# Two linked layers on one Trainium2 core: one of four weight sums per block-product group made in place by an adding transfer

## The chip, the core and the metric

The kernel runs on one core of a Trainium2 chip. Times are device microseconds (us) of one execution, without the host; lower is better. TensorE is called PE here, VectorE DVE, ScalarE ACT, GpSimd POOL and SyncE SP, as in the profile.

## The reference, cut to what matters

All of it is float32: 256 tokens of width 2048 go through a pooling mixer, a latent attention mixer, a hybrid mixer, a cross attention and a convolved feed-forward layer, one after the other, with norms and gates between. The change touches three of the many products with a weight matrix from memory:

```
out = (mixed * scale * silu(g)) @ pool_w_out        # 4096 x 2048, "pool_out"
out = (o * silu(g)) @ mla_w_out                     # 2048 x 2048, "mla_out"
out = (silu(conv(gate)) * val) @ w_down             # 5504 x 2048, "down"
```

## The kernel before, in words

**Products in three passes.** Each float32 weight tile is split into a high part (ACT copies it to float32r, w_hi) and a low part (DVE: raw - w_hi, w_lo). PE forms y_hi w_hi + y_hi w_lo + y_lo w_hi (function times, lines 961 to 965). A *unit* is a 512 KB tile of weights: two k tiles of 128 rows by 512 columns. SP loads units into the ring raw of 8 slots, each when the slot's last reader is done: it waits on w_lo for the product number that the table RELEASED gives (line 653). The rings w_hi and w_lo have 4 slots (RING), so ACT and DVE are at most four products ahead of PE.

**Groups of block products.** In the three products above a part of the inner dimension is done in groups: four units (B11, B12, B22, B21; two pairs of k tiles by two column chunks) meet a 2 x 2 block of the activations, and seven block products, each of half a plain unit's PE work, take the place of eight (Strassen's scheme in Winograd's form). That needs four sums of activations, made once, and four sums of weight tiles per group. In before, all four weight sums are DVE subtractions in place in raw (step_lo, lines 2465, 2467, 2469 and 2473), mixed with the seven low parts. ACT waits for each sum with w_sums (summed, line 1799). The block products go in the order B11, B22, T1, T3, B21, T2, T4 (function quad, line 1013; the names of the four sums are those of the change). Their results go into banks e1, e5, e6, e7 and the banks of the chunks; quads_mixed and quads_out add them up at the end of a pair of chunks.

There are 16 groups: 6 in pool_out (three per pair of chunks), 2 in mla_out and 8 in down (four per pair). The tables POOL_OUT, MLA_OUT and DOWN set the order: ten plain units stand before the first group of pool_out and of down, three before that of mla_out; between groups stand three plain units in pool_out, two in mla_out and four in down.

**POOL's queue.** layer_end(n) (line 3591) waits (n = 0: until PE has done eight products of pool_out; n = 1: attention heads done), loads post_gain (1024 KB), waits for it, and multiplies each chunk of the mixer's output by it when the chunk's squares are summed; for n = 1 it issues the loads of mem_features and mem_tokens (2048 KB each) at its first chunk. At the end of the kernel POOL waits for up, loads final_gain and multiplies the finished chunks. It is otherwise idle in these stages.

Of the kernel before, what the change touches and what calls it, by code (L numbers as in the profile page):

```python
# [71 lines left out]

POOL_QUADS = [20, 24, 28]
P0, P1, P2, P3 = ([("plain", c, (k, k + 1)) for k in range(0, 20, 2)] for c in range(NCH))
PQ = [[("quad", n, k)] for n, k in enumerate(POOL_QUADS)]
POOL_OUT = [P0[:9] + P1[:1] + PQ[0] + P1[1:4] + PQ[1] + P1[4:7] + PQ[2] + P1[7:] + P0[9:],
            P2[:4] + PQ[0] + P2[4:7] + PQ[1] + P2[7:9] + P3[:1] + PQ[2] + P2[9:] + P3[1:]]
# [3 lines left out]
D0, D1, D2, D3 = ([("plain", c, kts) for kts in DOWN_WHOLE] for c in range(NCH))  # L81
DOWN_ENDING = DOWN_WHOLE[-RING:]
DQ = [[("quad", n, k)] for n, k in enumerate(DOWN_QUADS)]
DOWN = [D0[:10] + DQ[0] + D1[:4] + DQ[1] + D1[4:8] + DQ[2] + D1[8:12] + DQ[3] + D1[12:] + D0[10:],
        D2[:4] + DQ[0] + D2[4:8] + DQ[1] + D2[8:12] + DQ[2] + D3[:4] + DQ[3] + D2[12:] + D3[4:]]
# [5 lines left out]
M2, M3 = ([("plain", c, (k, k + 1)) for k in range(0, 8, 2)] for c in (2, 3))  # L91
MQ = [[("quad", n, k)] for n, k in enumerate(MLA_OUT_QUADS)]
MLA_OUT = [[], M2[:3] + MQ[0] + M3[:2] + MQ[1] + M2[3:] + M3[2:]]


def quad_tables(first_unit, pairs, before):

    loads, released, quads_end, plain_end = [], [], [], {}
    last_quad = 0
    products = first_unit + before  # L100
    for p, steps in enumerate(pairs):
        for kind, c, kts in steps:
            if kind == "plain":
                loads.append((kts, c))
                released.append(products)
                products += 1
                plain_end[c] = products
            else:
                j1, j2 = (kts, kts + 1), (kts + 2, kts + 3)
                loads += [(j1, 2 * p), (j1, 2 * p + 1), (j2, 2 * p + 1), (j2, 2 * p)]  # L110
                released += [products + 3, products + 3, products + 5, products + 6]
                products += 7
                last_quad = products
        quads_end.append(last_quad)
    return loads, released, quads_end, plain_end
# [3 lines left out]
POOL_LOADS, POOL_RELEASED, POOL_QUADS_END, POOL_PLAIN_END = quad_tables(UNITS_END["pool"], POOL_OUT, 0)  # L119
SINCE_MLA_OUT = SINCE_POOL_OUT + 3 * len(MLA_OUT_QUADS)  # L120
MLA_OUT_PAIR = UNITS_END["heads"] + 16
MLA_OUT_LOADS, MLA_OUT_RELEASED, MLA_OUT_QUADS_END, MLA_OUT_PLAIN_END = quad_tables(MLA_OUT_PAIR, MLA_OUT, SINCE_POOL_OUT)
DOWN_LOADS, DOWN_RELEASED, DOWN_QUADS_END, DOWN_PLAIN_END = quad_tables(UNITS_END["up"], DOWN, SINCE_MLA_OUT)
# [8 lines left out]
assert POOL_RELEASED[-RAW:] == [UNITS_END["pool_out"] + SINCE_POOL_OUT - RAW + n for n in range(RAW)]  # L132
# [126 lines left out]
def build(nc, a, out):  # L259
# [191 lines left out]
    class Paired:  # L451

        def __init__(self, name, y, yh, yl, tiles, sums, sums_hi, sums_lo, quads, steps, loads, quads_end, plain_end, pairs_before):
# [3 lines left out]
            self.steps, self.loads, self.quads_end, self.plain_end, self.pairs_before = steps, loads, quads_end, plain_end, pairs_before  # L457
            self.both = len(steps[0]) > 0
# [13 lines left out]
        def blocks(self, j, tt):  # L472
# [10 lines left out]
    pool_out = Paired("pool_out", y32, yh, yl, POOL_Y, psums, psums_hi, psums_lo, POOL_QUADS, POOL_OUT, POOL_LOADS,  # L483
                      POOL_QUADS_END, POOL_PLAIN_END, 0)
    down = Paired("down", fy, fyh, fyl, DOWN_Y, fsums, fsums_hi, fsums_lo, DOWN_QUADS, DOWN, DOWN_LOADS,
                  DOWN_QUADS_END, DOWN_PLAIN_END, 3)
    msums, msums_lo, msums_hi = (arena(f"mla_y_sums{n}", off, [128, 4, len(MLA_OUT_QUADS), 2, 128], dt)
                                 for n, off, dt in (("", 81920, F32), ("_lo", 81920, F32R), ("_hi", 90112, F32R)))
    mla_out = Paired("mla_out", None, xh, xl, [], msums, [msums_hi[:, m] for m in range(4)], msums_lo, MLA_OUT_QUADS, MLA_OUT,
                     MLA_OUT_LOADS, MLA_OUT_QUADS_END, MLA_OUT_PLAIN_END, 1)  # L490
# [228 lines left out]
    def _(pe):  # L719
# [238 lines left out]
        pe.wait_ge(S("ident_in"), 16)  # L958
# [8 lines left out]
        def paired(x, split, ending=()):  # L967

            def pair(p):
# [21 lines left out]
                def plain(c, kts):  # L991
# [3 lines left out]
                    for n, k in enumerate(kts):  # L995
                        cols = slice(n * 512, n * 512 + 512)
                        for tt in range(2):
                            tok = slice(tt * 128, tt * 128 + 128)
                            last = times(x.bank(c, tt), x.yh[:, k, tok], x.yl[:, k, tok], wh[:, cols], wl[:, cols],
                                         begins((c, tt)), (c, kts) == final[c] and n == len(kts) - 1)  # L1000
# [3 lines left out]
                def block(dst, name, yh_, yl_, final=False):  # L1004

                    wh, wl = weight_slot()
                    for n in range(2):
                        cols = slice(n * 512, n * 512 + 512)
                        last = times(dst, yh_[:, n], yl_[:, n], wh[:, cols], wl[:, cols], n == 0 and begins(name), final and n == 1)
# [3 lines left out]
                def quad(q, k):  # L1013

                    e1, e5, e6, e7 = x.quad_banks(p)
                    c, last = 2 * p, q == len(x.quads) - 1
                    y_ready(k)
                    y1, y2 = slice(k, k + 2), slice(k + 2, k + 4)
                    t0, t1 = slice(0, 128), slice(128, 256)
                    block(e1, "e1", x.yh[:, y1, t0], x.yl[:, y1, t0], last)  # L1020
                    block(x.bank(c + 1, 0), (c + 1, 0), x.sums_hi[2][:, q], x.sums_lo[:, 2, q])
                    if x.both:
                        block(e5, "e5", x.yh[:, y1, t1], x.yl[:, y1, t1], last)
                    else:
                        block(e5, "e5", x.sums_hi[3][:, q], x.sums_lo[:, 3, q], last)
                    block(e7, "e7", x.sums_hi[0][:, q], x.sums_lo[:, 0, q], last)
                    block(x.bank(c, 0), (c, 0), x.yh[:, y2, t0], x.yl[:, y2, t0])
                    block(e6, "e6", x.sums_hi[1][:, q], x.sums_lo[:, 1, q], last)
                    block(x.bank(c, 1), (c, 1), x.yh[:, y2, t1], x.yl[:, y2, t1])
                    t.add("unit", 4)  # L1030
                    t.add("more", -4)
# [31 lines left out]
                final = {c: (c, kts) for kind, c, kts in x.steps[p] if kind == "plain"}  # L1063
# [8 lines left out]
                steps = x.steps[p][:-len(ending)] if p == 1 and ending else x.steps[p]  # L1072
                for kind, c, kts in steps:
                    if (kind == "quad" or c == 2 * p + 1) and begins("all sets"):
                        for s in range(2):
                            pe.wait_ge(S(f"mm_free{s}"), t.at(f"set{s}", 1))
                    if kind == "plain":
                        plain(c, kts)
                    else:
                        if c == 0 and not x.both:  # L1080
                            pe.wait_ge(S(split), len(POOL_Y) + 1)
                        elif c == 0 and p == 0:
                            pe.wait_ge(S(split), x.tiles.index("sums") + 1)
                        quad(c, kts)
# [516 lines left out]
    def _(act):  # L1601
# [191 lines left out]
        def loaded(n, cols=1024):  # L1793

            u = t.n["unit"] + n
# [3 lines left out]
        def summed(n, k):  # L1799

            act.wait_ge(S("w_sums"), t.n.get("w_sums", 0) + k)
            return raw[:, (t.n["unit"] + n) % RAW, :]

        def step_hi(kind, kts):

            if kind == "plain":
                product_hi(loaded(0, 512 * len(kts)))
                t.add("unit")
                t.add("more", -1)
            else:  # L1810
                product_hi(loaded(0))
                product_hi(loaded(2))
                product_hi(summed(0, 1))
                product_hi(summed(1, 2))
                product_hi(loaded(3))
                product_hi(summed(2, 3))
                product_hi(summed(3, 4))
                t.add("unit", 4)
                t.add("more", -4)
                t.add("w_sums", 4)  # L1820
# [86 lines left out]
        for n, (kind, _, kts) in enumerate(POOL_OUT[0]):  # L1907
            if n >= 6:
                step_hi(kind, kts)
# [10 lines left out]
        for n, (kind, _, kts) in enumerate(POOL_OUT[1]):  # L1920
            step_hi(kind, kts)
# [175 lines left out]
        for n, (kind, _, kts) in enumerate(MLA_OUT[1]):  # L2097
            if n >= LEAD:
                step_hi(kind, kts)
# [288 lines left out]
        for n, (kind, _, kts) in enumerate(DOWN[0]):  # L2388
            if n >= 6:
                step_hi(kind, kts)  # L2390
            if n in DOWN_Y_STEPS:
                y_hi(DOWN_Y_STEPS[n])
        for n, (kind, _, kts) in enumerate(DOWN[1]):
            step_hi(kind, kts)
# [26 lines left out]
    def _(dve):  # L2421
# [32 lines left out]
        def step_lo(kind, kts):  # L2454

            u = t.n["unit"]
            if kind == "plain":
                product_lo(raw[:, u % RAW, 0:512 * len(kts)])
                t.add("unit")
                t.add("more", -1)  # L2460
                return
            b11, b12, b22, b21 = (raw[:, (u + n) % RAW, :] for n in range(4))
# [1235 lines left out]
```

## Time and profile before

| | |
|---|---|
| median of 3 runs | 2436.18 us (2436.09 to 2437.14) |
| profiled execution, first to last instruction (span) | 2434.2 us |
| its own time outside the span | not listed apart; the median lies 2.0 us above the span |
| PE / DVE / ACT / POOL busy | 100% / 71% / 56% / 3% of the span |
| HBM traffic over the span | 185 GB/s |
| granted PE clock | 0.999 |

A row of the profile's groups reads: line, engine, operation, output <- inputs, shapes, count | busy us, mean ns of one | idle time of the engine before them and what ended it. A time in a timeline counts from the start of the span, and a DMA's time to landing from its issue. PE's matmuls overlap in the pipeline, so the mean of one is longer than the distance between two. PEld is the weight load, which overlaps PE.

### The profile page before, as it was taken

The numbers are of one execution on the slowest core, as the hardware profiler recorded it, in microseconds if no ns is written. First come the engines' busy times: TensorE is split into PE (matmuls) and PEld (weight loads), VectorE is DVE, ScalarE is ACT, GpSimd is POOL, SyncE is SP. The second block draws the span as 40 slices with busy tenths as digits, with TensorE's granted clock in tenths as the row PEclk, the third lists the DMA queues.
The fourth block names the chain that finished last, engine by engine and source line by source line (L and its number), as shares of the span: only waits on it lengthen the run. The fifth ranks groups of instructions, "written<-read, shape, count | busy, mean of one in ns | idle before, by whom it ended". The sixth has DMA issues, their size and how long they took to land.

```text
span 2434.2 us, 33996 instructions
## 1 busy us (share of the span) xinstructions
PE 2423.9 (100%) x12679; PEld 2084.6 (86%) x12679; DVE 1720.3 (71%) x2083; ACT 1373.7 (56%) x1823; POOL 64.7 (3%) x79
## 2 busy tenths in 40 slices
PE   9999999999999999999999999999999999999998
PEld 8888888888889999888888888888988888888887
DVE  7675757899765656796756667665767657679887
ACT  6444444556656666565755556565644545455555
POOL 0000000001100000010000000000000000000001
PEclk9999999999999999999999999999999999999999
DMA  8666666565555554565585554454565565656654
GB/s 314 199 189 185 188 189 183 188 218 199 180 175 181 179 158 147 211 212 189 165 235 163 161 171 151 164 178 154 172 191 180 189 190 180 191 169 205 220 184 145
DMA packets 234595, 453.03 MB, mean 186 GB/s; under 512 B 14929, under 2 KB 60417, under 8 KB 233324
## 3 DMA queue, kind: packets, MB, share of 16 engines
q1 hardware_dynamic: 230960, 435.94, 55.9%
q0 software_dynamic: 3120, 14.90, 1.7%
q10 hardware_dynamic: 396, 0.59, 0.2%
q8 instruction: 75, 1.23, 0.2%
q14 instruction: 44, 0.36, 0.0%
HBM read 448.68 MB, written 2.69 MB: 185 GB/s over the span
## 4 chain that ended last, share of the span: by engine, by line
PE 99%; DVE 1%; ACT 0%; issue 0%; ACTq 0%; DVEq 0%
PE ps L813 25%; PE ps L815 13%; PE ps L779 12%; PE ps L781 12%; PE ps L780 12%; PE ps L963 6%; PE ps L964 6%; PE ps L965 6%; PE ps L737 1%; PE ps L844 1%; PE ps L846 1%; PE ps L845 1%; PE ps L1443 1%; PE ps L1214 0%; PE ps L1202 0%; PE ps L1401 0%
## 5 line engine op out<-in xcount | busy, mean ns | idle before, releaser
L2443 DVE TENSOR_TENSOR w_lo<-raw,w_hi 128x1024 fp32r<-128x1024 f32 x689 | 842.1, 1228 | 466.7 <-ACT w_hi L1613 446.8
L1613 ACT ACTIVATE w_hi<-raw 128x1024 fp32r<-128x1024 f32 x689 | 726.8, 1060 | 650.9 <-PE ps L815 357.7
L813 PE MATMUL ps<-x_hi_lo,w_hi 128*128 128x512 f32 x2336 | 821.0, 394 | 0.0
L815 PE MATMUL ps<-x_hi_lo,w_lo 128*128 128x256 f32 x2336 | 660.7, 283 | 0.0
L813 PEld LDWEIGHTS ps<-x_hi_lo,w_hi 128*128 128x128 f32 x2336 | 438.8, 188 | 101.2
L779 PE MATMUL ps<-w_hi,x_hi_lo 128*128 128x512 f32 (+3 forms) x1184 | 461.9, 390 | 0.0
L781 PE MATMUL ps<-w_hi,x_hi_lo 128*128 128x512 f32 (+3 forms) x1184 | 453.7, 383 | 0.0
L780 PE MATMUL ps<-w_lo,x_hi_lo 128*128 128x512 f32 (+3 forms) x1184 | 452.7, 382 | 0.0
L815 PEld LDWEIGHTS ps<-x_hi_lo,w_lo 128*128 128x128 f32 x2336 | 439.3, 188 | 0.0
L1790 ACT ACTIVATE w_hi<-raw 128x1024 fp32r<-128x1024 f32 (+1 forms) x201 | 209.4, 1051 | 169.8 <-PE ps L965 152.2
L2451 DVE TENSOR_TENSOR w_lo<-raw,w_hi 128x1024 fp32r<-128x1024 f32 (+1 forms) x201 | 243.2, 1228 | 35.4 <-ACT w_hi L1790 35.1
L781 PEld LDWEIGHTS ps<-w_hi,x_hi_lo 128*128 128x128 f32 x1184 | 222.5, 188 | 39.1
L779 PEld LDWEIGHTS ps<-w_hi,x_hi_lo 128*128 128x128 f32 x1184 | 222.8, 188 | 36.5 <-issue 1.2
L780 PEld LDWEIGHTS ps<-w_lo,x_hi_lo 128*128 128x128 f32 x1184 | 222.9, 188 | 35.9
L964 PE MATMUL ps<-w_lo,ffn_y_hi 128*128 128x512 f32 (+1 forms) x283 | 111.0, 392 | 0.0
L965 PE MATMUL ps<-w_hi,ffn_y_lo 128*128 128x512 f32 (+1 forms) x283 | 111.0, 392 | 0.0
L963 PE MATMUL ps<-w_hi,ffn_y_hi 128*128 128x512 f32 (+1 forms) x283 | 111.0, 392 | 0.0
L813 PE MATMUL ps<-pooled_hi_lo,w_hi 128*128 128x512 f32 x256 | 90.0, 393 | 0.0
L963 PE MATMUL ps<-w_hi,pool_y_hi 128*128 128x512 f32 x208 | 82.3, 396 | 0.0
L964 PE MATMUL ps<-w_lo,pool_y_hi 128*128 128x512 f32 x208 | 82.1, 395 | 0.0
L965 PE MATMUL ps<-w_hi,pool_y_lo 128*128 128x512 f32 x208 | 82.1, 395 | 0.0
L815 PE MATMUL ps<-pooled_hi_lo,w_lo 128*128 128x256 f32 x256 | 72.4, 283 | 0.0
(469 smaller groups left out, 2711.9 us busy)
## 6 DMA issues: line engine op xcount, KB each, us to landing
raw<-in_w_up SPq DMA_DIRECT2D x160, 512.0 KB, 3.9
raw<-in_pool_w_in SPq DMA_DIRECT2D x126, 512.0 KB, 3.8
raw<-in_w_in SPq DMA_DIRECT2D x96, 480.0 KB, 3.8
raw<-in_w_down SPq DMA_DIRECT2D x84, 512.0 KB, 5.1
raw<-in_pool_w_out SPq DMA_DIRECT2D x64, 512.0 KB, 4.8
raw<-in_ple_w_gate SPq DMA_DIRECT2D x64, 512.0 KB, 4.3
raw<-in_mla_w_in SPq DMA_DIRECT2D x56, 448.0 KB, 3.5
raw<-in_pool_w_group SPq DMA_DIRECT2D x32, 512.0 KB, 4.1
```

The costliest lines, as they stand in the source:

```text
L779: pe.matmul(dst, xhi[:, k, tok], wh, start=k == units[0][0], stop=False)
L780: pe.matmul(dst, xhi[:, k, tok], wl, start=False, stop=False)
L781: last = pe.matmul(dst, xlo[:, k, tok], wh, start=False, stop=k == units[-1][-1])
L813: pe.matmul(bank, w_hi[:, slot, cols], xs[:, k].rearrange("p s n -> p (s n)"), start=k == 0, stop=False, skip_group_check=True)
L815: last = pe.matmul(bank[:, 0:T], w_lo[:, slot, cols], xs[:, k, 0, :], start=False, stop=k == nkt - 1, skip_group_check=True)
L963: pe.matmul(dst, yh_, wh, start=first, stop=False)
L964: pe.matmul(dst, yh_, wl, start=False, stop=False)
L965: return pe.matmul(dst, yl_, wh, start=False, stop=final)
L1613: act.activation(w_hi[:, t.slot(), :], raw[:, slot, :], ACT.Copy).then_inc(S("w_hi"), 1)
L1790: act.activation(w_hi[:, t.slot(), 0:cols], src, ACT.Copy).then_inc(S("w_hi"), 1)
L2443: dve.tensor_tensor(w_lo[:, t.slot(), :], raw[:, u % RAW, :], w_hi[:, t.slot(), :].bitcast(F32), ALU.subtract)\
L2451: dve.tensor_tensor(w_lo[:, t.slot(), 0:cols], src, w_hi[:, t.slot(), 0:cols].bitcast(F32), ALU.subtract).then_inc(S("w_lo"), 1)
```

## The change

Per group, the sum of the first row's two tiles, B12 + B11, is made by a DMA on POOL's queue that adds tile B11 into tile B12 (weight_sums; issued when both tiles have landed and the adding transfer before has too; its landing counts w_added). DVE makes the other three sums; it waits for w_added after the low part of B22, and ACT waits for it before T1's high part. SP loads B12 ahead of B11. The block products go B11, B22, T1, B21, T3, T2, T4. Signs of activation sums and of the final additions are turned to fit. The causal mask's load shares a semaphore with the identity's, so PE and DVE wait for both. The lists of steps are flattened to one entry per block product. weight_sums stands behind the load of post_gain in layer_end (for pool_out and for mla_out) and behind the load of final_gain (for down). The diff, cut:

```diff
+PARTS = ("B11", "B22", "T1", "B21", "T3", "T2", "T4")
+SLOT_OF = {"B12": 0, "T1": 0, "B11": 1, "T3": 1, "B22": 2, "T2": 2, "B21": 3, "T4": 3}
+LAST_USE = ("T1", "T3", "T2", "T4")
...
+def quads_at(first_tiles):
+
+    return [[(part, n, k) for part in PARTS] for n, k in enumerate(first_tiles)]
...
-                loads += [(j1, 2 * p), (j1, 2 * p + 1), (j2, 2 * p + 1), (j2, 2 * p)]
-                released += [products + 3, products + 3, products + 5, products + 6]
...
+                loads += [(j1, 2 * p + 1), (j1, 2 * p), (j2, 2 * p + 1), (j2, 2 * p)]
+                released += [at[part] for part in LAST_USE]
...
-        pe.wait_ge(S("ident_in"), 16)
+        pe.wait_ge(S("ident_in"), 32)
...
+                    if name == "B11":
+                        y_ready(k)
+                        t.add("unit", 4)
+                        t.add("more", -4)
+                        block(i, e1, "e1", x.yh[:, y1, t0], x.yl[:, y1, t0])
+                    elif name == "B22":
+                        block(i, x.bank(c + 1, 0), (c + 1, 0), x.sums_hi[2][:, q], x.sums_lo[:, 2, q])
+                    elif name == "B21":
+                        block(i, x.bank(c, 0), (c, 0), x.yh[:, y2, t0], x.yl[:, y2, t0])
+                    elif name == "T1" and x.both:
+                        block(i, e5, "e5", x.yh[:, y1, t1], x.yl[:, y1, t1])
+                    elif name == "T1":
+                        block(i, e5, "e5", x.sums_hi[3][:, q], x.sums_lo[:, 3, q])
+                    elif name == "T3":
+                        block(i, e7, "e7", x.sums_hi[0][:, q], x.sums_lo[:, 0, q])
+                    elif name == "T2":
+                        block(i, e6, "e6", x.sums_hi[1][:, q], x.sums_lo[:, 1, q])
...
+        def step_hi(entry):
+
+            for kind, _, kts, u in entry:
+                if kind == "plain":
+                    product_hi(loaded(u, 512 * len(kts)))
+                elif kind in ("B11", "B22", "B21"):
+                    product_hi(loaded(u + SLOT_OF[kind]))
+                else:
+                    if kind == "T1":
+                        act.wait_ge(S("w_added"), 16 * (t.n.get("quad", 0) + 1))
+                    else:
+                        act.wait_ge(S("w_sums"), 3 * t.n.get("quad", 0) + {"T2": 1, "T3": 2, "T4": 3}[kind])
+                    product_hi(raw[:, (u + SLOT_OF[kind]) % RAW, :])
...
-            product_lo(b11)
-            dve.wait_ge(S(f"raw_full{(u + 1) % RAW}"), 16 * ((u + 1) // RAW + 1))
-            dve.tensor_tensor(b11, b12, b11, ALU.subtract).then_inc(S("w_sums"), 1)
-            product_lo(b22)
-            dve.tensor_tensor(b12, b22, b12, ALU.subtract).then_inc(S("w_sums"), 1)
-            product_lo(b11)
-            dve.tensor_tensor(b22, b22, b11, ALU.subtract).then_inc(S("w_sums"), 1)
-            product_lo(b12)
-            product_lo(b21)
-            dve.wait_ge(S("w_sums"), t.n.get("w_sums", 0) + 3)
-            dve.tensor_tensor(b21, b21, b22, ALU.subtract).then_inc(S("w_sums"), 1)
-            product_lo(b22)
...
+                b12, b11, b22, b21 = (raw[:, (u + n) % RAW, :] for n in range(4))
+                product_lo(raw[:, (u + SLOT_OF[kind]) % RAW, :])
+                if kind == "B22":
+                    dve.wait_ge(S("w_added"), 16 * (t.n.get("quad", 0) + 1))
+                    dve.tensor_tensor(b22, b22, b12, ALU.add).then_inc(S("w_sums"), 1)
+                elif kind == "T1":
+                    dve.wait_ge(S("w_sums"), 3 * t.n.get("quad", 0) + 1)
+                    dve.tensor_tensor(b11, b22, b11, ALU.subtract).then_inc(S("w_sums"), 1)
+                elif kind == "T3":
+                    dve.tensor_tensor(b21, b21, b22, ALU.add).then_inc(S("w_sums"), 1)
...
+        def weight_sums(x):
+
+            for u in x.weight_sums:
+                b12, b11 = (raw[:, (u + n) % RAW, :] for n in range(2))
+                for v in (u, u + 1):
+                    pool.wait_ge(S(f"raw_full{v % RAW}"), 16 * (v // RAW + 1))
+                if t.n["quad"]:
+                    pool.wait_ge(S("w_added"), 16 * t.n["quad"])
+                pool.dma_start(b12, b11, accum_op=ALU.add).then_inc(S("w_added"), 16)
+                t.add("quad")
...
             load(pgain, a["post_norm"][n:n + 1, :].broadcast_to([128, D]), "post_gain_in")
+            weight_sums(mla_out if n else pool_out)
             pool.wait_ge(S("post_gain_in"), 16 * (n + 1))
...
         products(pool, "up")
         load(fgain, a["norm_final_2"].unsqueeze(0).broadcast_to([128, D]), "final_gain_in")
+        weight_sums(down)
         pool.wait_ge(S("final_gain_in"), 16)
...
-                step(dve.tensor_tensor(o1[1], o1[0], e6, ALU.add))
+                step(dve.tensor_tensor(o1[1], e6, o1[0], ALU.subtract))
```

## Rows read from the trace of the kernel before

**Rows 1.** The page: span, busy time and share by engine.
```profile
span 2434.2 us, 33996 instructions
...
PE 2423.9 (100%) x12679; PEld 2084.6 (86%) x12679; DVE 1720.3 (71%) x2083; ACT 1373.7 (56%) x1823; POOL 64.7 (3%) x79
```

**Rows 2.** Paired stages in windows: us, busy by engine, clock, DMA share, GB/s.
```profile
457.00:632.00 175.00, 175.00 (x754) 141.41 (x753) 156.78 (x158) 100.39 (x110) 12.71 (x8) 1.00 0.61 206
...
2197.00:2427.00 230.00, 229.80 (x1000) 186.57 (x998) 201.22 (x190) 129.00 (x140) 9.77 (x7) 1.00 0.56 187
```

**Rows 3.** Line L963 by source: what its engine sat idle for.
```profile
its engine sat idle before it (us, times) until:
  DVE w_lo L2451: 0.4, 1
  DVE w_lo L2443: 0.3, 1
```

**Rows 4.** DVE groups by shape: line, op, count, busy us, mean ns, idle.
```profile
L2465 DVE TENSOR_TENSOR raw<-raw 128x1024 f32<-128x1024 f32 x16 | 19.5, 1218 | 0.0
```

**Rows 5.** DVE's timeline over the first group: start us, us, line, count.
```profile
479.61 2.35 DVE L2451 TENSOR_TENSOR w_lo<-raw,w_hi 128x1024 fp32r<-128x1024 f32 x2
...
483.01 1.22 DVE L2451 TENSOR_TENSOR w_lo<-raw,w_hi 128x1024 fp32r<-128x1024 f32 x1
484.15 1.22 DVE L2467 TENSOR_TENSOR raw<-raw 128x1024 f32<-128x1024 f32 x1
...
494.45 1.22 DVE L2451 TENSOR_TENSOR w_lo<-raw,w_hi 128x1024 fp32r<-128x1024 f32 x1
```

**Rows 6.** PE's weight loads there: first for T1, first after the group.
```profile
488.40 0.19 PEld L963 LDWEIGHTS ps<-w_hi,pool_y_hi 128*128 128x128 f32 x1
...
495.73 0.19 PEld L963 LDWEIGHTS ps<-w_hi,pool_y_hi 128*128 128x128 f32 x1 [0.37 <-DVE w_lo L2451]
```

**Rows 7.** POOL's timeline: start us, us, line, and idle before.
```profile
480.69 0.53 POOL L3589 DMA_DIRECT2D post_gain<-in_post_norm  x1 [450.10 <-PE ps L965]
...
1009.02 0.54 POOL L3589 DMA_DIRECT2D post_gain<-in_post_norm  x1
1019.49 0.53 POOL L3589 DMA_DIRECT2D mem_features<-in_mem_features  x1 [9.94 <-ACT mixer_out L1710]
```

**Rows 8.** DMA issues, to landing (us): at 480.6, 1009 and 1024; all.
```profile
post_gain<-in_post_norm POOLq DMA_DIRECT2D x1, 1024.0 KB, 7.0
...
post_gain<-in_post_norm POOLq DMA_DIRECT2D x1, 1024.0 KB, 4.9
...
raw<-in_mla_w_out SPq DMA_DIRECT2D x5, 512.0 KB, 10.3
...
raw<-in_w_down SPq DMA_DIRECT2D x84, 512.0 KB, 5.1
raw<-in_pool_w_out SPq DMA_DIRECT2D x64, 512.0 KB, 4.8
...
mem_features<-in_mem_features POOLq DMA_DIRECT2D x1, 2048.0 KB, 8.3
...
final_gain<-in_norm_final POOLq DMA_DIRECT2D x1, 1024.0 KB, 8.3
...
hybrid_qk_T<-junk POOLq DMA_DIRECT2D x16, 1.0 KB, 1.5
```

**Rows 9.** Two groups later in down: DVE timeline, then a PE weight load.
```profile
2347.05 1.23 DVE L2451 TENSOR_TENSOR w_lo<-raw,w_hi 128x1024 fp32r<-128x1024 f32 x1 [0.17 <-ACT w_hi L1790]
...
2362.14 1.22 DVE L2467 TENSOR_TENSOR raw<-raw 128x1024 f32<-128x1024 f32 x1
...
2367.78 0.19 PEld L963 LDWEIGHTS ps<-w_hi,ffn_y_hi 128*128 128x128 f32 x1
```

**Rows 10.** DVE's timeline in mla_out's pair.
```profile
1045.59 1.22 DVE L2451 TENSOR_TENSOR w_lo<-raw,w_hi 128x1024 fp32r<-128x1024 f32 x1
...
1059.03 1.22 DVE L2451 TENSOR_TENSOR w_lo<-raw,w_hi 128x1024 fp32r<-128x1024 f32 x1
```

More of the change, by code:

```diff
@@ L90 @@
 MLA_OUT_QUADS = [8, 12]
[L91 to L98, printed above, removed]
+M2, M3 = ([plain(c, (k, k + 1)) for k in range(0, 8, 2)] for c in (2, 3))
+MQ = quads_at(MLA_OUT_QUADS)
+MLA_OUT = [[], M2[:3] + MQ[:1] + M3[:2] + MQ[1:] + M2[3:] + M3[2:]]
@@ L99, in quad_tables, with paired_tables @@
+def paired_tables(first_unit, pairs, before):
+    loads, released, quads_end, plain_end, steps, units = [], [], [], {}, [], []
     last_quad = 0
     products = first_unit + before
-    for p, steps in enumerate(pairs):
-        for kind, c, kts in steps:
+    for p, pair in enumerate(pairs):
+        steps.append([])
+        for entry in pair:
+            unit = first_unit + len(loads)
+            steps[-1].append([(kind, c, kts, unit) for kind, c, kts in entry])
+            at = {kind: products + n for n, (kind, _, _) in enumerate(entry)}
+            products += len(entry)
+            kind, c, kts = entry[0]
@@ L131 @@
 assert all(r <= UNITS_END["mla_out"] + SINCE_MLA_OUT - RAW + n for n, r in enumerate(MLA_OUT_RELEASED[-RAW:]))
-assert POOL_RELEASED[-RAW:] == [UNITS_END["pool_out"] + SINCE_POOL_OUT - RAW + n for n in range(RAW)]
+assert all(r <= UNITS_END["pool_out"] + SINCE_POOL_OUT - RAW + n for n, r in enumerate(POOL_RELEASED[-RAW:]))
 HEAD_CHUNKS = [("gate", 3), ("k", 0), ("v", 0), ("k", 1), ("gate", 4), ("v", 1), ("k", 2), ("gate", 5), ("v", 2),
@@ L1061, in turned_ending @@
                     t.add("unit", len(ending))
-                final = {c: (c, kts) for kind, c, kts in x.steps[p] if kind == "plain"}
+                banks = {"B11": ["e1"], "T1": ["e5"], "T2": ["e6"], "T3": ["e7"], "B22": [(2 * p + 1, 0)], "B21": [(2 * p, 0)], "T4": [(2 * p, 1)]}
+                parts = [at for entry in x.steps[p] for at in entry]
+                closing = {bank: i for i, (kind, c, _, _) in enumerate(parts) for bank in banks.get(kind, [(c, 0), (c, 1)])}
                 if p == 0:
@@ L1071, in pair @@
                     pe.wait_ge(S(f"mm_free{s}"), t.at(f"set{s}", 1))
-                steps = x.steps[p][:-len(ending)] if p == 1 and ending else x.steps[p]
-                for kind, c, kts in steps:
-                    if (kind == "quad" or c == 2 * p + 1) and begins("all sets"):
+                steps = parts[:-len(ending)] if p == 1 and ending else parts
+                for i, (kind, c, kts, _) in enumerate(steps):
+                    if (kind != "plain" or c == 2 * p + 1) and begins("all sets"):
                         for s in range(2):
@@ L1077, in pair @@
                     if kind == "plain":
-                        plain(c, kts)
+                        plain(i, c, kts)
                     else:
-                        if c == 0 and not x.both:
+                        if kind == "B11" and c == 0 and not x.both:
                             pe.wait_ge(S(split), len(POOL_Y) + 1)
-                        elif c == 0 and p == 0:
+                        elif kind == "B11" and c == 0 and p == 0:
                             pe.wait_ge(S(split), x.tiles.index("sums") + 1)
-                        quad(c, kts)
+                        part(i, kind, c, kts)
                 if p == 1 and ending:
@@ L1919, in _ @@
                 y_hi(n - 4)
-        for n, (kind, _, kts) in enumerate(POOL_OUT[1]):
-            step_hi(kind, kts)
+        for n, entry in enumerate(pool_out.steps[1]):
+            step_hi(entry)
             if n == 15:
@@ L2925, in _ @@
             quads_mixed(0, n)
-        for n, (kind, _, kts) in enumerate(POOL_OUT[1]):
-            step_lo(kind, kts)
+        for n, entry in enumerate(pool_out.steps[1]):
+            step_lo(entry)
             if n == 1:
@@ L3536, in _ @@
                 quads_out(0, n - 28)
-        for n, (kind, _, kts) in enumerate(DOWN[1]):
-            step_lo(kind, kts)
+        for n, entry in enumerate(down.steps[1]):
+            step_lo(entry)
             if n == 0:
```

175 lines of the change are left out of this document (75 added, 100 removed).

## The prediction

> **What bounds the kernel now.** I read the page first: TensorE (PE) is busy for 2423.9 of the 2434.2 us span [rows 1]. A share of 100% alone does not prove a bound, since matmuls are pipelined, so I looked next at the stages that the change touches. In the windows of pool_out and down, PE is busy all the time at a granted clock of 1.00, VectorE (DVE) 157 of 175 us and 201 of 230 us, the DMA engines 0.61 and 0.56 [rows 2]. Then I asked what the product line L963 waited for: 0.7 us in the whole kernel, both waits for w_lo from DVE [rows 3]. So PE sets the end, and the work that the change takes from DVE lies beside PE. The most that it can give back is the 0.7 us of waits. Everything that makes a product's weights late, on the other hand, is paid in full, because PE never catches up.
>
> **The change, part by part.** *Removed:* one of the four DVE sums in each of the 16 groups, 16 x 1.218 = 19.5 us of DVE [rows 4]. All of it lies under PE's matmuls. Worth on the path: the 0.37 us stall before the first unit behind group 1 [rows 6], perhaps; its cover is PE's own work. The swapped signs of the sums and the wait on the identity's semaphore are the same operations: nothing.
>
> *Order.* B21 now comes before T3 on PE, ACT and DVE, seven products as before. On SP the slots come free after products 2, 4, 5 and 6 instead of 3, 3, 5 and 6. The slot of T1 is free a product earlier, the next one a product later. The second slot is where the next group's second tile goes in down, so this sits inside the window reckoned below; otherwise I put it at zero.
>
> *Added:* 16 transfers on POOL's DMA queue, each adding one 512 KB tile into another, and three kinds of waits: POOL for both tiles (and the transfer before), ACT and DVE for the landing. Behind DVE's wait stands all that PE needs: the T2 sum, then the low parts of T1, B21, T3 and so on. The question for each group is whether the transfer lands in time.
>
> *Group 1 of pool_out* is the special one. POOL reaches its first transfer only when eight products of pool_out are done, and behind the load of post_gain, which is issued at 480.69 and takes 0.53 us to issue [rows 7]. Both tiles have then long landed. This post_gain is 1024 KB and lands 7.0 us after its issue [rows 8], at 487.7. The adding transfer is issued at about 481.2 on the same queue, and I take it to move after post_gain. When is it needed? DVE has done B11 and B22 low by 483.1 (in before, B22's began at 483.01 behind one sum that now is gone [rows 5]). From the landing X DVE then has, before the first whole unit behind the group, ten operations: sum, T1, sum, B21, T3, sum, T2, T4, a y part, the unit. They follow each other at 484.15 - 483.01 = 1.14 us [rows 5]. With 0.2 us for the semaphore, the last end and PE, that unit starts at X + 11.6. In before it started at 495.73 [rows 6]. So the loss is X - 484.1. (The nearer product T1, first weights at 488.40 [rows 6], needs only X + 2.5, so the end of the group decides.)
>
> *X.* No accumulating transfer is in the trace. mem_features (2048 KB) landed in 8.3 us and the second post_gain (1024 KB) in 4.9 [rows 8]: one more MB costs 3.4 us. An adding transfer reads two tiles and writes one. Counted as half a MB it costs 1.7 us behind post_gain, as 1.5 MB 5.1 us. I take 2.5 us, between 1.7 and the 3.4 of one MB, because SP's queue runs dry while DVE waits (DVE frees the slots). X = 490.2, loss 6.1 us. Ends: 489.4 gives 5.3 and 492.8 gives 8.7.
>
> Behind that rests the order on the queue. The Trainium skill (DMA: Bandwidth & Descriptors, "Two DMAs through the same engine are not ordered") says that inside one queue of one engine descriptors start in order, though completion isn't guaranteed in order. By that rule the transfer can't begin before post_gain's pieces; here no row shows two such transfers well enough to prove it. The same page ("Anatomy of one DMA") fits 2.0 us + bytes/436 GB/s, an estimate of 3.2 us for 512 KB. By that alone X would be 484.4 and the loss 0.3 us; but its 4.4 us for 1 MB is below both post_gain rows, 7.0 and 4.9.
>
> *The other 15 groups.* In down, a group's second tile can be asked for when T3's low part of the group before is done, 2347.05 + 1.23 = 2348.3 [rows 9], and lands 5.1 us later, at 2353.4. T1's first weights are loaded at 2367.78 [rows 9], so X may be 2365.3. The unit behind the group starts five products later; those take 495.73 - 0.37 - 488.40 = 6.96 us [rows 6], so at 2374.7. It wants nine DVE operations (no y part), 10.5 us, so X may be 2364.2: a window of 10.8 us. DVE itself would wait from 2362.1 on without harm. POOL-queue transfers took 1.5 us (1 KB) to 8.3 us (1 MB, final_gain; or 2 MB) [rows 8], an adding one estimated at 4 to 8. Cost taken: nothing; end: see the rivals. In down's first group the transfer stands behind final_gain (8.3 us [rows 8], from 2198), but is wanted only after ten units of PE work.
>
> *mla_out.* POOL now issues the two memory loads (mem_features was issued at 1019.49 [rows 7]) only after the second group's tiles have landed; no row here says when, I take the time of T1's low part in the first group, 1045.6 [rows 10], 26 us later. They slow the weight loads: five landed in 10.3 us under them [rows 8]. The tile B22 of the second group can be asked for at T1's low part, 1045.59 + 1.22 = 1046.8, lands at 1057.1, and its own low part starts at 1059.03, 1.1 us after ScalarE needs the tile [rows 10]. It fits by 0.8 us, with PE several products behind; taken at nothing, at most 2 us.
>
> **Sum.** +6.1 us, the 0.37 us stall already inside. The profiled execution's span is 2434.2 us; the runs' median of 2436.18 lies 2.0 us above it, which is taken as unchanged around the span. Forecast 2436.2 + 6.1 = **2442.3 us**, 0.25% slower. About 0.2%, 4.9 us, is what a measurement of this kernel can tell from no change; that is crossed at X = 489.0.
>
> **The rivals.**
> A, the forecast: the transfer waits behind post_gain. 2441.5 to 2444.9. Chance 0.60.
> B, not slower: the transfer in group 1 shares the queue with post_gain or post_gain is quicker, so that it lands before 489.0. Place: the first DVE wait. A 512 KB load takes 4.8 us [rows 8]: X = 486.0, loss 1.9 us, 2438.1; at 484.1 nothing is left and the 0.4 us stall comes back, 2435.8. For it: the second post_gain took 4.9 instead of 7.0. Against: then X would still be 485.6 + 2.5 = 488.1, a loss of 4.0. It decides from X < 489.0. Chance 0.22.
> C, an adding transfer needs more than the 10.8 us window. Then every group stalls. At 15 us: 15 x 4.2 = 63 us and some 16 us in group 1, 2515 us. Just at the window group 1 alone costs X = 487.7 + 9, so 12.6 us, 2448.8; that is where C begins. For it: nothing shows the adding rate; against: at 3.4 us a MB the window holds 3 MB. Chance 0.12.
> D, the forecast, and mla_out's moved burst costs 2 to 5 us more: 2444 to 2449. Chance 0.06.
> That the sum isn't taken from DVE at all would be seen at once; it has no chance by the diff.
>
> **How the numbers follow.** Slower: nearly all of A (0.53), C and D, 0.71. Same: the low edge of A and B, 0.27. Faster, which only more than the waits of rows 3 could give, 0.02. The range reaches from the middle of B, 2437.6, to the end of D and the beginning of C, 2449; it leaves out half of B and most of C.
>
> **What would show it.** Right: PE idle for about 6 us in all near 488 to 502, released by w_lo; the DVE sum that follows B22 waits there for a POOL DMA; the first adding transfer lands 8 to 12 us after its issue, the others in 4 to 8, without a PE wait in down. DVE busy falls by 19.5 us. Wrong: no PE wait at group 1, or PE waits once in every group (C), or around 1057 to 1065 (D).

## The result, and the profile after

| | before | after |
|---|---|---|
| median of five runs each, same chip | 2436.57 us (2436.09 to 2437.14) | 2446.49 us (2446.14 to 2447.03) |
| ratio after/before | | 1.0041 [1.0028, 1.0053] |
| profiled span | 2434.2 us | 2444.6 us |

Slower by 9.9 us, 0.4%, against a forecast of 6.1 us. The span tells the same, 10.4 us, and what lies around it has not changed (1.9 us between span and median; 2.0 before). One execution of the experiments' kernels, at a granted clock of 0.80, took 2779 us and is left out of its kernel's median. The page of after, span and busy times:

```profile
span 2444.6 us, 34012 instructions
PE 2428.0 (99%) x12679; PEld 2085.6 (85%) x12679; DVE 1702.4 (70%) x2067; ACT 1373.0 (56%) x1823; POOL 78.8 (3%) x95
```

Beside [rows 1], DVE has 17.9 us less to do and the span is 10.4 us longer. (The forecast said 19.5 us less. One sum takes 1.22 us, but they start 1.14 us apart, so the busy time falls by about 1.14 each, 18.2 in all.) PE, which sets the end, ran the same number of matmuls. The waits of PE (total us, times, longest) begin in before with this line:

```profile
PE ps L954 <- DVE ones_square L2608: 2.1, 1, 2.1
```

In after one line stands ahead of it:

```profile
PE ps L984 <- DVE w_lo L2475: 6.2, 5, 4.6
PE ps L975 <- DVE ones_square L2629: 2.1, 1, 2.1
```

**Where the 10.4 us are.** To place them I split the span at three rows of the tiles' view, the first and last product on pool_y_hi and the first on ffn_y_hi: pool_out, all that lies between pool_out and down, and down to the end. Before: 457.8 to 627.8 and 2197.9. After: 457.9 to 635.3 and 2208.4. So pool_out takes 177.4 instead of 170.0 us (+7.4), the middle 1573.1 instead of 1570.1 (+3.0), and down to the end 236.2 instead of 236.3. Most of this is the group that the prediction charged, and one place that it did not.

**Group 1 of pool_out.** POOL's timeline of after from 480 us (start, us, engine, line, what, idle before and what ended it), and the DMAs issued at 481.2 to 481.3 with those that the same answer lists (KB each, us to landing):

```profile
480.71 0.54 POOL L3610 DMA_DIRECT2D post_gain<-in_post_norm  x1 [450.26 <-PE ps L986]
481.25 0.90 POOL L3620 DMA_DIRECT2D raw<-raw  x1
```

```profile
post_gain<-in_post_norm POOLq DMA_DIRECT2D x1, 1024.0 KB, 6.9
...
raw<-raw POOLq DMA_DIRECT2D x1, 512.0 KB, 9.7
```

Post_gain lands at 487.6, the adding transfer at 490.9. The chain that ended last, of the stretch 484 to 500, walks from there to PE:

```profile
481.25 9.68 DMA raw<-raw
490.93 0.02 issue
490.96 1.22 DVE raw L2490
492.18 1.15 DVE w_lo L2475
493.33 0.04 issue
493.37 0.80 PE ps L984
494.17 0.43 PE ps L985
...
498.43 0.31 PE ps L986
498.75 0.23 PE ps L984
```

PE's first weights after the wait, and the unit behind the group, from PEld's timeline:

```profile
493.37 0.29 PEld L984 LDWEIGHTS ps<-w_hi,pool_y_hi 128*128 128x128 f32 x1 [5.03 <-DVE w_lo L2475]
...
502.61 0.19 PEld L984 LDWEIGHTS ps<-w_hi,pool_y_hi 128*128 128x128 f32 x1
```

PE gets no weights for 5.0 us (its matmuls stand still for 4.6 us, the wait listed above), and the unit that in before was loaded at 495.73 [rows 6] comes at 502.6, 6.9 us later. The chain shows something else: behind the idle time one matmul follows the other after 0.43 us, not 0.23. The windows say why (us, busy times of PE, PEld, DVE, ACT, POOL, then the granted clock as a share of full speed, DMA share, GB/s):

```profile
480.00:488.00 8.00, 8.00 (x36) 6.49 (x35) 3.15 (x3) 1.06 (x1) 1.44 (x2) 1.00 0.71 214
488.00:493.00 5.00, 0.78 (x4) 0.29 (x2) 2.04 (x2) 2.00 (x2) 0.00 (x0) 0.87 0.42 95
493.00:498.00 5.00, 4.63 (x11) 3.70 (x12) 5.00 (x6) 2.04 (x3) 0.29 (x1) 0.50 0.34 109
498.00:505.00 7.00, 7.00 (x31) 5.64 (x30) 7.00 (x7) 6.72 (x7) 0.58 (x1) 0.96 0.97 244
2208.00:2437.00 229.00, 229.00 (x996) 186.08 (x995) 192.03 (x181) 128.51 (x138) 16.65 (x15) 1.00 0.67 205
```

Until 488 PE worked at the upper of its two levels (2.4 GHz); after the idle time it works at 0.50 of it (1.2 GHz) from 493 to 498. That costs little here. PE's own way to the unit behind the group is 493.37 + 6.96 us, and some 2.4 more for 4.8 us at half clock, 502.7; DVE's ten operations give 490.93 + 11.6 = 502.5.

**A slower pace behind it.** Pool_out loses 7.4 us and the unit behind the group only 6.9. The other 0.5 us come evenly up to the stage's end: seven plain units in a row take 19.60 us instead of 19.52 (first weights at 541.74 and 561.34; in before at 534.64 and 554.16). The runs show just these two paces. From the second unit behind group 1 to the last one the stage takes 127.4 us in after and in the kernels of the next section called "DVE makes the sum", "memory loads early" and "transfers of down delayed"; it takes 126.9 us in before and in the other seven. The kernel without any transfer is among the slower ones, and most of those with transfers are not. So these 0.5 us are no cost of the transfers; what sets the pace stays open.

The last of the windows above is down: PE is busy all the time. Its seven later groups' adding transfers land in time, though only just (POOL's view of tile raw, 2240 to 2440):

```profile
DMA to landing us min/median/max: 8.2/9.7/10.1
```

**mla_out.** POOL, after, second group of mla_out:

```profile
1051.77 0.89 POOL L3610 DMA_DIRECT2D mem_features<-in_mem_features  x1
1052.31 1.06 POOL L3610 DMA_DIRECT2D mem_tokens<-in_mem  x1
1053.04 2.90 POOL L3645 TENSOR_TENSOR mixer_out<-mixer_out,post_gain 128x512 f32<-128x512 f32 x2
```

Two things meet the group there. A low part on DVE that starts beside POOL's multiplications takes 3.89 us instead of 1.22, and a weight load asked for behind the two memory loads takes 12.0 us, so that ACT waits for it (timelines of DVE and ACT, and the DMAs issued from 1057.0 to 1057.2):

```profile
1053.15 3.89 DVE L2475 TENSOR_TENSOR w_lo<-raw,w_hi 128x1024 fp32r<-128x1024 f32 x1 [0.43 <-ACT w_hi L1819]
...
1069.12 1.06 ACT L1819 ACTIVATE w_hi<-raw 128x1024 fp32r<-128x1024 f32 x1 [3.44 <-DMA raw<-in_mla_w_out]
```

```profile
raw<-in_mla_w_out SPq DMA_DIRECT2D x1, 512.0 KB, 12.0
```

PE loses the 3.0 us in small gaps: at four places from 1058 to 1080 the next weights come some 0.8 us later than the 0.23 us in which they otherwise follow. The first and the third, from PEld's timeline:

```profile
1059.36 0.19 PEld L984 LDWEIGHTS ps<-w_hi,x_hi_lo 128*128 128x128 f32 x1 [0.87 <-DVE w_lo L2475]
...
1076.03 0.19 PEld L984 LDWEIGHTS ps<-w_hi,x_hi_lo 128*128 128x128 f32 x1 [0.80 <-DVE w_lo L2475]
```

The two effects are linked: the weight load goes into the slot that this slow low part frees at 1057.04, so it is asked for 2.7 us late and then takes longer. Both effects could be read in before, where they met no group: the memory loads went out at 1019.49 [rows 7], and DVE's low part beside POOL's multiplication was as slow.

```profile
1020.44 3.93 DVE L2443 TENSOR_TENSOR w_lo<-raw,w_hi 128x1024 fp32r<-128x1024 f32 x1 [0.25 <-ACT w_hi L1613]
...
1020.73 1.31 POOL L3612 TENSOR_TENSOR mixer_out<-mixer_out,post_gain 128x512 f32<-128x512 f32 x1
```

### The profile page after: what moved, and what is told of

It reads as the page before. It is cut to its first block, busy times and chain, and to the rows that moved or that the text cites. A ratio compares the mean times of both kernels' runs of the same rounds, so it can differ in the third digit from the quotient of the medians.

```text
span 2444.6 us, 34012 instructions
## 1 busy us (share of the span) xinstructions
PE 2428.0 (99%) x12679; PEld 2085.6 (85%) x12679; DVE 1702.4 (70%) x2067; ACT 1373.0 (56%) x1823; POOL 78.8 (3%) x95
## 4 chain that ended last, share of the span: by engine, by line
PE 78%; issue 19%; DMA 1%; DVE 1%; ACT 1%; POOL 0%; SPq 0%; ACTq 0%; DVEq 0%; POOLq 0%
PE ps L834 12%; PE ps L800 12%; PE ps L802 12%; PE ps L801 12%; PE ps L836 6%; PE ps L984 5%; PE ps L985 5%; PE ps L986 5%; PE ps L758 1%; PE ps L867 1%; PE ps L865 1%; PE ps L866 1%; DVE w_lo L2475 1%; PE ps L1472 1%; DMA raw<-in_mla_w_out 0%
```

## The experiments

My theory: the place of the transfers on POOL's queue costs the time, +7.4 us for the first one behind post_gain and +3.0 us for the work that the mla_out transfers delay. The rivals: the new order of products costs it; DVE or the number of DMAs costs it everywhere. All kernels start from after; those called "first early" have that edit as well. "(one)" is a single execution, whose stretches are then the evidence. "pool", "middle" and "down" are the three stretches, less those of before.

| run | median us, or one run | span | pool | middle | down |
|---|---|---|---|---|---|
| after | 2446.49 | 2444.6 | +7.4 | +3.0 | -0.1 |
| first transfer early | 2439.07 | 2437.1 | -0.2 | +3.3 | -0.1 |
| first transfer just ahead of post_gain | 2442.59 (one) | 2440.7 | +3.5 | +3.0 | -0.1 |
| DVE makes the sum | 2436.02 | 2434.9 | +0.6 | +0.1 | -0.1 |
| memory loads early | 2443.7 (one) | 2441.9 | +7.5 | +0.9 | -0.1 |
| multiplication early | 2446.78 (one) | 2444.9 | +8.2 | +2.3 | 0.0 |
| copy in place of addition | 2443.33 (one) | 2441.5 | +5.4 | +1.8 | -0.1 |
| transfers of down delayed | 2452.61 (one) | 2450.8 | +7.6 | +3.0 | +5.7 |
| first early, multiplication early | 2438.62 | 2436.5 | -0.1 | +2.5 | -0.1 |
| first early, memory loads early | 2437.19 | 2435.0 | -0.1 | +0.8 | -0.1 |
| all three early | 2436.07 | 2434.1 | -0.1 | 0.0 | 0.0 |

**The first transfer ahead of everything in POOL's pool_out part.**

```diff
             if n == 0:
+                weight_sums(pool_out, slice(0, 1))
                 products(pool, "pool", 8)
             ...
-            weight_sums(mla_out if n else pool_out)
+            weight_sums(mla_out if n else pool_out, slice(0 if n else 1, None))
```

> Only pool_out's first adding transfer is moved: it goes ahead of POOL's wait for eight products of pool_out and of the load of post_gain. Theory Q (that one transfer comes late, behind post_gain): it lands at about 475 us, PE has no stall near 488, the half clock of 493 to 498 is gone, and the 7.4 us that pool_out lost come back; the 2.9 us lost later in mla_out stay: about 2439 us. Rival R (the adding transfers and the new order as such cost time in pool_out): 2444 us or more, with the loss spread over the six groups.

Measured: 2439.07 us, ratio to before 1.0012 [1.0003, 1.0022]. The transfer is issued at 467.44, when its tiles have landed, and lands 6.5 us later. The stretch of pool_out is as in before, and the granted clock stays at 1.00 from 485 to 500. What stays on PE are the small waits of mla_out:

```profile
PE ps L984 <- DVE w_lo L2475: 1.7, 4, 0.6
```

So what group 1 costs is all this one transfer's place: 6.9 of the 7.4 us, the rest being the pace.

**Behind the eight products, but ahead of post_gain.** This splits that place into its two causes, the wait for PE's products and the load in front.

```diff
                 products(pool, "pool", 8)
+                weight_sums(pool_out, slice(0, 1))
```

(and the rest of the groups behind post_gain, as above)

> pool_out's first adding transfer stays behind the wait for eight products but goes ahead of the load of post_gain. By the queue's order it then lands 5 to 6.5 us after its issue at 480.7, X = 486 to 487, and by loss = X - 484.1 pool_out loses 2 to 3 us instead of 7.4; a PE gap of about 1 us is too short to bring the half clock, or brings less of it: span 2440. If the order on the queue does not matter, X stays near 490.9 and the span at 2444.6.

Measured: pool +3.5 us. The DMAs of this kernel issued from 480.7 to 481.4:

```profile
post_gain<-in_post_norm POOLq DMA_DIRECT2D x1, 1024.0 KB, 8.7
raw<-raw POOLq DMA_DIRECT2D x1, 512.0 KB, 6.9
```

Issued at 480.76, the transfer lands at 487.6; X - 484.1 gives 3.5 us, as measured (I had expected 2 to 3). Now the addition lands in 6.9 us and post_gain in 8.7; behind post_gain it was 9.7 and 6.9. Of these two, whichever is issued first lands first. So of group 1's 6.8 us, 3.3 came from standing behind post_gain and 3.5 from being issued only when eight products are done. PE's waits are short here (at most 1.2 us), and in the window 488 to 499 the granted clock stays at 1.00.

**The sum back on DVE, in the new order.** No transfers at all; in the new order DVE makes B12 + B11 behind the low part of B11.

```diff
+                if kind == "B11":
+                    dve.wait_ge(S(f"raw_full{u % RAW}"), 16 * (u // RAW + 1))
+                    dve.tensor_tensor(b12, b12, b11, ALU.add).then_inc(S("w_added"), 1)
...
-            weight_sums(mla_out if n else pool_out)
...
-        weight_sums(down)
```

> The new order of products, of tiles and of slots and the turned signs are kept, but DVE makes the first sum of each group again and POOL issues no adding transfer. If the whole loss comes from the transfers (Q and what POOL's queue does in mla_out): as before, 2436 to 2437 us. If the order itself costs (R): some of the 10 us stays.

Measured: 2436.02 against 2436.16 us, ratio 1.000 [0.999, 1.001]. The order of the products, the slots' release and the changed signs cost nothing that can be measured; its +0.6 us in pool_out is the slower pace. The first rival falls.

**The memory loads ahead of mla_out's transfers.**

```diff
+            if n == 1:
+                chunk_out(pool, "mla_out", 0)
+                load(memf, a["mem_features"], "mem_in")
+                load(memt, tokens(a["mem_2"][0]), "mem_in")
             weight_sums(mla_out if n else pool_out)
...
-                if n == 1 and c == 0:
-                    load(memf, a["mem_features"], "mem_in")
-                    load(memt, tokens(a["mem_2"][0]), "mem_in")
```

> As the changed kernel, but the loads of mem_features and mem_tokens are issued ahead of mla_out's two adding transfers, as before; the multiplication by post_gain stays behind them. If the moved loads cause the second pair of stalls (PE gaps at 1075 and 1078, 1.1 us together), these go and the first pair (1058 and 1062, 1.2 us) stays, with one low part of DVE still at 3.9 us: the span is 1 us shorter than the changed kernel's 2444.6. If the loads cause all of it, 2.3 us shorter; if nothing, the same.

Measured: middle +0.9 instead of +3.0 us, so 2.1 of the 3.0 us go with the loads, more than the 1 us of the theory. Of the four gaps one of 1.0 us is left, at 1061.

**The multiplication of chunk 0 ahead of them.**

```diff
-            weight_sums(mla_out if n else pool_out)
             pool.wait_ge(S("post_gain_in"), 16 * (n + 1))
+            if n == 1:
+                chunk_out(pool, "mla_out", 0)
+                for tt in range(2):
+                    last = pool.tensor_tensor(outt[:, tt, 0:512], outt[:, tt, 0:512], pgain[:, 0:512], ALU.mult)
+                last.then_inc(S("post_gained"), 1)
+            weight_sums(mla_out if n else pool_out)
...
+                if n == 1 and c == 0:
+                    continue
```

> As the changed kernel, but POOL multiplies mla_out's chunk 0 by post_gain ahead of the two adding transfers, as before; the memory loads stay behind them. If POOL's multiplication holds DVE (a low part of 3.9 us instead of 1.2), that low part is 1.2 us again, the first pair of PE gaps goes, and the tile B22 of the second group is asked for 2.7 us earlier, so that the second pair shrinks or goes too: the span is 1.2 to 2.3 us shorter than 2444.6. If the memory loads are the whole cause, nothing changes.

Measured: 2446.78 us, the middle at +2.3, but pool at +8.2. The edit did more than I meant: the wait for post_gain now stands ahead of pool_out's transfers too.

```profile
487.90 0.88 POOL L3620 DMA_DIRECT2D raw<-raw  x1 [6.51 <-DMA post_gain<-in_post_norm]
```

Issued at 487.90, it lands 4.5 us later, at 492.41, and X - 484.1 = 8.3 us: a fourth point on the line of the prediction, got by mistake. The run's time alone says nothing on the multiplication, so I repeated both edits clean, on the kernel with the first transfer early.

> On top of e1 (pool_out repaired, 2439.07): POOL multiplies mla_out's chunk 0 ahead of the two adding transfers, the memory loads stay behind them. In the run before this one (e4) the same edit also held pool_out's first transfer back; here it cannot. Theory: the loads make tile B22 of the second group late whether or not DVE was held before, so the first pair of PE gaps goes and the second stays or grows: 2438 to 2439. If POOL's hold on DVE were the root of both pairs: 2436.2.

> On top of e1: the memory loads go ahead of mla_out's adding transfers, the multiplication stays behind them. Theory: B22 of the second group comes in time, and only POOL's hold on DVE is left, which falls beside another group: one PE gap of under 1 us, 2437. If the loads were the whole cause: 2436.2. If the multiplication were: 2439.

Measured: with the multiplication early 2438.62 us (ratio 1.001 [1.0, 1.002]), middle +2.5; with the loads early 2437.19 us (ratio 1.0005 [0.9995, 1.0015]), middle +0.8. In the first, the memory loads still go out behind the transfers. Its weight load asked for at 1046.9, and PE's waits:

```profile
raw<-in_mla_w_out SPq DMA_DIRECT2D x1, 512.0 KB, 14.1
...
PE ps L984 <- DVE w_lo L2475: 1.2, 3, 0.6
```

In the second, the multiplication still meets a low part (DVE's timeline), and one wait is left:

```profile
1048.49 1.81 DVE L2475 TENSOR_TENSOR w_lo<-raw,w_hi 128x1024 fp32r<-128x1024 f32 x1 [0.43 <-ACT w_hi L1819]
...
PE ps L984 <- DVE w_lo L2475: 0.6, 1, 0.6
```

So the loads, moved into the group, cost 2.5 us and the multiplication 0.8; 3.3 together, which is the middle of the kernel with only the first transfer early. That the two add up is partly chance, for each edit also moves the rest: in the first the weight load takes 14.1 us instead of 12.0, and in the second POOL's two multiplications (1047.31 to 1051.46) meet two low parts, the one shown and the next, which take 4.04 us together instead of 2.4. The 0.8 us is read from the trace; the runs alone do not tell it from nothing.

**All three early.**

> The changed kernel with all three repairs: pool_out's first transfer ahead of post_gain, and mla_out's memory loads and first multiplication ahead of its adding transfers. Theory (PE sets the end, DVE's 19.5 us are worth at most the 0.4 us wait at 495.7): 2436.2 us, no difference from before that can be measured. Rival: the relief of DVE is worth something once the stalls are gone: 2434 us or less.

Measured over five rounds: 2436.07 us (2435.38 to 2437.4) against 2436.02, ratio 1.000 [0.9991, 1.0009]. PE's list of waits has no w_lo any more:

```profile
PE ps L975 <- DVE ones_square L2629: 2.1, 1, 2.1
PE ps L800 <- ACT ple_proj L1739: 0.6, 1, 0.6
```

The whole loss goes when three things on POOL's queue are put right. DVE keeps its 17.7 us less work (1702.6 us busy), and they buy nothing. No kernel here is faster than before.

**A copy in place of the addition.** T1 then holds B11 alone: the addition is left out of the computation.

```diff
-                pool.dma_start(b12, b11, accum_op=ALU.add).then_inc(S("w_added"), 16)
+                pool.dma_start(b12, b11).then_inc(S("w_added"), 16)
```

> Every adding transfer is a plain copy of tile B11 into B12: the addition is left out of the transfer. It measures what adding costs over copying. Adding in the transfer cheap: landings as with it (6.5 us in pool_out, 9.8 us in down). Adding dear: 3.5 to 5 us. In group 1, behind post_gain, X would fall from 490.9 to about 489 and the loss to 5 us.

Measured: pool +5.4 us; the first lands at 489.58 (X - 484.1 = 5.5). Its seven later transfers of down:

```profile
L3620 POOL DMA_DIRECT2D raw<-raw x7: 527/527/530, 2241.4 to 2380.8; - x7
...
DMA to landing us min/median/max: 6.5/7.3/8.4
```

Against 9.7 us with the addition, adding costs about 2.4 us per 512 KB more than copying at the median, and POOL spends 0.85 us instead of 0.53 to issue it. In down most of the 9.7 us is therefore there without the addition. In pool_out's five later groups copies took 4.1 to 5.6 us and adding transfers 6.5 to 7.4. The middle falls to +1.8; which of its two parts gains was not told apart.

**How near the edge down is.** Ahead of each later transfer of down the final_gain load (1024 KB) is repeated, so that the transfer stands behind it.

```diff
+                if x is down and t.n["quad"] > 8:
+                    pool.wait_ge(S("final_gain_in"), 16 * (t.n["quad"] - 8))
+                    load(fgain, a["norm_final_2"].unsqueeze(0).broadcast_to([128, D]), "final_gain_in")
                 pool.dma_start(b12, b11, accum_op=ALU.add).then_inc(S("w_added"), 16)
```

(and DVE's and POOL's waits for final_gain count all eight loads)

> In down, ahead of each adding transfer but the first, POOL loads the 1 MB of final_gain again on the same queue, which makes the transfer later by 3 to 5 us. By the window of 10.8 us that I worked out, transfers that land 9.8 us after their tiles would then land at 13 to 15 and PE would stall 2 to 4 us in each of the seven groups: 15 to 30 us more in down. If the window is wider than I think, nothing happens.

Measured: down +5.7 us. The transfers and PE's waits in down:

```profile
DMA to landing us min/median/max: 10.6/11.3/12.3
...
PE ps L984 <- DVE w_lo L2475: 3.0, 7, 0.5
```

With 0.5 us for the issue of the load in front, the sum is there 11.1 to 12.8 us after the tiles. PEld's timeline shows gaps behind five of the seven groups, whose transfers were issued at 2266.8, 2288.8, 2345.0, 2368.1 and 2390.1 (11.7 to 12.8 us). The group at 11.1 us shows none. Nor does the first group of the second pair of chunks (issued at 2322.8, 11.8 us): more plain units stand ahead of it, and DVE waits only 0.9 us for its sum. The delay came out smaller than I wanted (1.6 us at the median, 2.1 with the issue), and so did the cost, 5.7 us instead of 15 to 30. The window is real, its edge between 11.1 and 11.7 us against the 10.8 worked out, and after uses 8.2 to 10.1 us of it. The repeated loads, 7 MB in all, are more traffic too (DMA share 0.74 instead of 0.67 from 2208 to 2437); how much of the cost is theirs was not told apart.

## Why the prediction was right in its main step, and wrong in others

The time lies in the range given, but the sum was short: 6.1 us against 9.9. The range held because it reached to the end of rival D, which had a chance of 0.06. Step by step:

**PE sets the end, DVE's sums lie beside it: right.** Shown from both sides: with the sums off DVE and nothing late the time is that of before (all three early), and with the sum put back on DVE in the new order too. The 0.37 us stall of [rows 6] went with the rest where the first transfer is early, as forecast, and is below what the runs resolve.

**Group 1 pays X - 484.1: right, and the size nearly so.**

| kernel | X | X - 484.1 | unit behind the group late by | pool_out longer by |
|---|---|---|---|---|
| just ahead of post_gain | 487.62 | 3.5 | 3.5 | 3.5 |
| copy | 489.58 | 5.5 | 5.4 | 5.4 |
| after | 490.93 | 6.8 | 6.8 | 7.4 |
| multiplication early (wait for post_gain in front) | 492.41 | 8.3 | 8.2 | 8.2 |

(The unit's lateness is counted here from the stage's first weights.) The reckoned need of ten DVE operations behind the landing holds to 0.1 us. X itself was forecast at 490.2 (487.7 + 2.5). Post_gain came at 487.6; the term that was mis-sized is the adding transfer behind it, 3.3 us instead of 2.5. I had taken 2.5 as lying between 1.7 and 3.4; the price of one MB was the nearer one. The rest of the 7.4 us, 0.5, is the slower pace, no part of this step.

The order on the queue rested on the Trainium skill (DMA: Bandwidth & Descriptors, "Two DMAs through the same engine are not ordered"): inside one queue descriptors start in order. The landings in the two orders of post_gain and the transfer agree with it: post_gain at 487.6 and the transfer at 490.9, or the transfer at 487.6 and post_gain, issued 481.32, at 490.0. The fit of the same page of the Trainium skill ("Anatomy of one DMA"), an estimate of 3.2 us for 512 KB, is too low here: the 16 transfers took 5.5 to 10.1 us, and the copies in down 6.5 to 8.4; only one copy, in mla_out, came under it with 2.9. The measurement decides.

**The other groups, "estimated at 4 to 8 ... Cost taken: nothing": right in its cost, wrong in its size.** They took 9.7 us at the median in down. The zero held by 0.7 us against the worked-out window of 10.8, and by 1.0 to 1.6 us against the measured one, so luck had a part in it. Rival C was much nearer than its chance of 0.12 makes it look: with the sum there some 2 us later, five of down's later groups stall.

**mla_out, "it fits by 0.8 us, with PE several products behind; taken at nothing, at most 2 us": wrong, this step failed.** It cost 3.0 us. Two things were missed. The load under the memory burst was put at the 10.3 us of [rows 8]. That is the median of five loads, some of which ran at the burst's end; the three asked for first in before, from 1024 to 1028.5, took 11.0 at the median. Here it takes 12.0, and 14.1 in the run with the multiplication early, and the cover of 0.8 us was gone. Second, I listed the DMAs that POOL is held back from, but not its multiplications, though the step I moved issues both. The row at 1020.44 in before shows their price, 2.7 us on DVE, in the very stretch I had read for the memory loads. Together they make the tile 4.4 us later than reckoned (2.7 of DVE, 1.7 of the load), against the cover of 0.8; PE pays 3.0 of it. The Trainium skill (SBUF — State Buffer, "Who interferes with whom") has the rule: a VectorE instruction with two SBUF inputs contends with a GpSimd instruction that reads SBUF, by a shared read port. The rows agree: the low part, with two inputs in SBUF, takes 3.89 or 3.93 us beside POOL's multiplication and 1.22 alone. It ends at 1057.04 in after, 1.1 us behind the end of POOL's second multiplication (1053.04 + 2.90 = 1055.94), as if it had stood still for both.

**The chances.** What happened is rival D on top of the forecast A: 7.4 + 3.0 against "6.1 and 2 to 5 more". It had 0.06, which was too little: a cover of 0.8 us was set against a load whose price was a median of unlike loads. The error of the span, 10.4 - 6.1 = 4.3 us, is these 3.0 us, 0.7 us of group 1 and the 0.5 us of pace.

**Left open.** Whether a transfer could be made quicker than the 8.2 to 10.1 us of down, and so the window wide enough for comfort; whether DVE's 17.7 us could pay for further groups of block products, which PE would gain from. Neither was tried. What sets the two paces of pool_out is open too.

## What to carry to other kernels

Work taken from an engine that PE hides is worth at most PE's waits for it (0.7 us here), while the transfer that takes its place has to be in time at every single use: find for each use when it is issued, what stands ahead of it on its queue, and how many operations follow its landing before PE needs the last of them. When a queue gets a new wait, price everything behind it, computations as well as loads: the order of three things on POOL's queue was all of the cost that runs can tell, and putting it right brought the time back to that of before, not below. For a cover of less than a microsecond take the slowest row of such a load, not the median.

## What the runs showed of the hardware

- **The granted clock fell while PE stood still.** No weights were loaded from 488.4 to 493.4; the granted clock was 0.50 from 492 to 498, matmuls 0.43 us apart instead of 0.23. In the kernel whose PE waits are 1.2 us at most, it stays at 1.00 from 488 to 499.
- **A low part on DVE is held by a multiplication on POOL** that it meets: 3.89 us instead of 1.22 beside two of them; where two low parts shared them, the two took 4.04 us instead of 2.4.
- **An adding transfer from SBUF to SBUF is slow for its size:** 512 KB in 5.5 to 10.1 us in after (median 7.8 us; 4.5 us once, with the wait for post_gain in front), and 0.85 us of POOL to issue. Loads of the same size from memory took 4.8 and 5.1 us [rows 8].
- **4 MB issued on POOL's queue** make the weight loads of SP's queue up to three times as long: 12.0 and 14.1 us in two kernels and 11.0 at the median of three in before, where before's load asked for between 1049 and 1050, clear of them, took 4.0.
- **Two paces of PE at a granted clock of 1.00:** seven plain units of pool_out in a row took 19.60 us in four kernels and 19.52 in the other eight; the edits do not explain which.
